# A hybrid decoder layer: the feed-forward products as seven block products in place of eight

## The reference

```python
def _swiglu(h, w_gate, w_up, w_down):
    return (jax.nn.silu(h @ w_gate) * (h @ w_up)) @ w_down

x = x + 1/2 * SwiGLU_1(RMSNorm(x))          # d_ff = 2816
x = x + token_mix(RMSNorm(x))               # RWKV-7 and mLSTM mixers, gates, W_out
x = x + cross_attention(RMSNorm(x), RMSNorm(mem))   # 4 heads, 256 memory tokens
x = x + 1/2 * SwiGLU_2(RMSNorm(x))
out = RMSNorm(x)
```

## Time and profile before

| | us |
|---|---|
| median of 3 runs | 2962.98 |
| the runs | 2962.14, 2962.98, 2966.65 |
| the profiled execution: its span (the page gives no other time for it) | 2967.3 |
| TensorE busy | 2849.2 |
| VectorE, GpSimd, ScalarE busy | 1354.6, 1246.7, 564.3 |
| first part, from the first matmul to its last | 12.3 to about 740.7 |
| second part | 2219.9 to 2939.3 |

### The profile page before, as it was taken

One profiled execution on the slowest core, in us unless ns is written; L12 is line 12 of the kernel. 1 busy time (PEld: TensorE's weight loads), 2 busy tenths in 40 slices (PEclk: granted clock), 3 DMA queues, 4 the chain that ended last, 5 costly groups with the idle time before them and its releaser, 6 DMA issues.

```text
span 2967.3 us, 36791 instructions
## 1 busy us (share of the span) xinstructions
PE 2849.2 (96%) x14694; PEld 2359.7 (80%) x14694; DVE 1354.6 (46%) x1109; ACT 564.3 (19%) x793; POOL 1246.7 (42%) x627
## 2 busy tenths in 40 slices
PE   7999999999999998999999999998899999999996
PEld 5888888888788877777777778888788888888885
DVE  5431331234556535776777555543344322331334
ACT  3100010012000112443444232214321100100011
POOL 3433344433694623555555443321043344433331
PEclk9999999999999999998999999999999999999998
DMA  3111111112762554444434164122011111111111
GB/s 133 43 50 50 50 49 45 48 46 103 298 247 92 192 194 149 101 107 139 102 102 104 61 223 149 51 75 102 8 43 50 49 50 47 46 49 50 50 41 73
DMA packets 115401, 271.35 MB, mean 91 GB/s; under 512 B 7644, under 2 KB 58972, under 8 KB 108272
## 3 DMA queue, kind: packets, MB, share of 16 engines
q1 hardware_dynamic: 93504, 210.79, 22.4%
q10 hardware_dynamic: 21808, 59.27, 5.3%
HBM read 207.56 MB, written 62.44 MB: 91 GB/s over the span
## 4 chain that ended last, share of the span: by engine, by line
PE 79%; issue 9%; POOL 6%; DVE 4%; ACT 1%; DMA 0%; SPq 0%; POOLq 0%; DVEq 0%; ACTq 0%
PE G L755 24%; PE G L757 24%; PE G L756 24%; PE G L879 2%; POOL AL L686 2%; PE G L1164 1%; PE G L916 1%; POOL Tr L680 1%; ACT sx L1559 0%; DVE nt_a L1644 0%; DVE mx L2008 0%; DVE px L2016 0%; POOL rho L669 0%; PE G L1156 0%; PE G L820 0%
## 5 line engine op out<-in xcount | busy, mean ns | idle before, releaser
L719 POOL TENSOR_TENSOR whi<-raw,zero 128x1024 fp32r<-128x1024 f32 (+1 forms) x199 | 378.2, 1900 | 1312.8 <-PE G L757 1233.2
L755 PE MATMUL G<-hhi,whi 128*128 128x512 f32 x2032 | 794.0, 391 | 21.0 <-DVE hlo L1650 17.9
L757 PE MATMUL G<-hhi,wlo 128*128 128x512 f32 x2032 | 791.8, 390 | 0.0
L756 PE MATMUL G<-hlo,whi 128*128 128x512 f32 x2032 | 791.5, 390 | 0.0
L722 POOL TENSOR_TENSOR wlo<-raw,whi 128x1024 fp32r<-128x1024 f32 (+1 forms) x199 | 482.6, 2425 | 15.6
L755 PEld LDWEIGHTS G<-hhi,whi 128*128 128x128 f32 x2032 | 382.1, 188 | 104.2 <-issue 13.0
L757 PEld LDWEIGHTS G<-hhi,wlo 128*128 128x128 f32 x2032 | 382.1, 188 | 79.8
L756 PEld LDWEIGHTS G<-hlo,whi 128*128 128x128 f32 x2032 | 382.2, 188 | 79.6 <-issue 0.7
L755 PE MATMUL G<-ahi,whi 128*128 128x512 f32 x960 | 374.8, 390 | 2.7 <-DVEq L457 2.7
L756 PE MATMUL G<-alo,whi 128*128 128x512 f32 x960 | 374.2, 390 | 0.0
L757 PE MATMUL G<-ahi,wlo 128*128 128x512 f32 x960 | 374.1, 390 | 0.0
(11 more groups left out here) (329 smaller groups left out, 3301.8 us busy)
## 6 DMA issues: line engine op xcount, KB each, us to landing
gw<-gw_d SPq DMA_DIRECT2D x32, 1024.0 KB, 5.3
raw<-in_wg SPq DMA_DIRECT2D x44, 512.0 KB, 3.2
raw<-in_wu SPq DMA_DIRECT2D x44, 512.0 KB, 3.3
raw<-in_wd SPq DMA_DIRECT2D x32, 512.0 KB, 3.3
gw_d<-gw SPq DMA_DIRECT2D x16, 1024.0 KB, 4.8
graw<-in_gates_in SPq DMA_DIRECT2D x16, 512.0 KB, 7.2
raw<-in_ml_in SPq DMA_DIRECT2D x16, 512.0 KB, 3.7
zml_d<-po ACTq DMA_DIRECT2D x16, 512.0 KB, 2.6
```

The costliest lines, as they stand in the source:

```text
L719: nc.gpsimd.tensor_tensor(whi[:, k, 0:w], raw[:, k, 0:w], zero[:].to_broadcast([P, w]), ALU.add).then_inc(hi_made, 1)
L755: nc.tensor.matmul(dst, wh, hi, start=start, stop=False)
L756: nc.tensor.matmul(dst, wh, lo, start=False, stop=False)
L757: return nc.tensor.matmul(dst, wl, hi, start=False, stop=stop)
```

## The change

Both feed-forward parts are rewritten; the rest is as it was, but for places of tiles and semaphores. Weights and tokens are cut into 2 x 2 blocks: a pair of output columns by a pair of input tiles for the weights (A11 to A22), a pair of input tiles by two halves of 512 tokens for the tokens (B11 to B22). Four block products of two terms each, eight products, become seven, of sums of blocks (the Winograd form of Strassen's scheme):

- weights: S1 = A21 + A22, S2 = S1 - A11, S3 = A11 - A21, S4 = A12 - S2, made by GpSimd (`sums`);
- tokens: T1 to T4, sums of the B blocks, made once a part by VectorE in the place of `xT`, and split into high and low like the rest (`opT`; B11, B21 and B22 are in `opB`);
- products: P1 = A11 B11, P2 = A12 B21, P3 = S4 B22, P4 = A22 T4, P5 = S1 T1, P6 = S2 T2, P7 = S3 T3. P1, P6, P7 and P4 follow one another in one PSUM bank, P5 and P3 in a second, P2 in a third; what is read in between is copied out by ScalarE (`pp1`, `pu2`, `pp5`). c11 = P1 + P2, c12 = (P1 + P6) + P5 + P3, c22 = (P1 + P6 + P7) + P5, c21 is what the first bank holds at the end.

The work goes by slots: 22 for gate and up (even: the gate of 256 columns of d_ff, odd: their up; each product has 4 tiles), then 24 for down (six parts of the d_ff pairs, `PARTS`, one pair in the first part and two in the others, times four pairs of output chunks). A slot's weights are one load of 1 MB for gate and up. Each weight block has one buffer: ScalarE rounds the high part after the slot before has used it, VectorE makes the low part (in down GpSimd does). The activations of a pair are seven tiles (three blocks and four sums), split into high and low, and are stored in DRAM (`act_d`, 1.8 MB each of high and low) and loaded again for down in time for their part, except for the last pair's. x is loaded again too (`tokens_back`), since T1 to T4 overwrote it; the second part stores it before.

The diff is cut to SP's and GpSimd's program, TensorE's order, ScalarE's high part and the copy of U2, and VectorE's low part, one down step and its order of work:

```diff
-FF_PARTS = (8, 8, 6)
+PAIRS = FFC // 2
+HK = KD // 2
+NA = 2 * PAIRS
+PARTS = (((0, 0),), ((1, 2), (10, 3)), ((2, 0), (3, 1)), ((4, 2), (5, 3)), ((6, 0), (7, 1)), ((8, 2), (9, 3)))
+NB = len(PARTS) * (KD // 2)
...
+    act_d = [dram(f"act_d{f}", [PAIRS, 2, P, 7, HALF]) for f in range(2)]
...
+            def pair_weights(g):
+                if g < NA:
+                    dst, src = flat(sraw[g % 2][:]), (wu if g % 2 else wg)[g // 2]
+                else:
+                    p, m = divmod(g - NA, HK)
+                    w = len(PARTS[p]) * P
+                    dst, src = rsum[g % 2][:, 0:4, 0:w], wd[p][m].rearrange("p (b c) -> p b c", b=4)
+                sp.dma_start(dst, src).then_inc(sraw_in[g % 2], 16)
+
+            def slot(q, n):
+                for part, dst in enumerate((slh[n], sll[n])):
+                    sp.dma_start(dst[:].rearrange("p b t -> p (b t)").bitcast(F32),
+                                 act_d[f][q, part].rearrange("p b t -> p (b t)")).then_inc(slot_in[n], 16)
+
+            def tokens_back(m):
+                sp.dma_start(xT[:, 2 * m:2 * m + 2, :], x_src[:, 2 * m:2 * m + 2, :]).then_inc(xs_in[m], 16)
+
...
+            for g in range(NA - 1):
+                sp.wait_ge(*w_lo.at(f"A22_{g}", f))
+                sp.wait_ge(sum_made, (n0 + g + 1) * 4)
+                if g + 2 == NA + 1:
+                    break
+                pair_weights(g + 2)
+                if g % 2 == 0 and g:
+                    j = g // 2 - 1
+                    sp.wait_ge(act_hi, f * 2 * PAIRS + 2 * j + 2)
+                    sp.dma_start(act_d[f][j, 0].rearrange("p b t -> p (b t)"),
+                                 flat(hiS[:]).bitcast(F32)).then_inc(hi_out, 16)
+                    sp.wait_ge(act_lo, f * 2 * PAIRS + 2 * j + 2)
+                    sp.dma_start(act_d[f][j, 1].rearrange("p b t -> p (b t)"),
+                                 vS[:, 1:8, :].rearrange("p b t -> p (b t)")).then_inc(lo_out, 16)
+            sp.wait_ge(hi_out, (f + 1) * (PAIRS - 1) * 16)
+            sp.wait_ge(lo_out, (f + 1) * (PAIRS - 1) * 16)
+            tokens_back(0)
+            sp.wait_ge(p_made[1], n0 + NA)
+            sp.wait_ge(p_made[2], n0 + NA)
+            slot(0, 0)
+            sp.wait_ge(p_made[6], n0 + NA)
+            pair_weights(NA + 1)
+            sp.wait_ge(act_made, (f + 1) * 3 * PAIRS - 1)
+            tokens_back(1)
+            sp.wait_ge(p_made[4], n0 + NA)
+            slot(1, 2)
+            sp.wait_ge(act_lo, (f + 1) * 2 * PAIRS)
+            for m in (2, 3):
+                tokens_back(m)
+            for g in range(NA, SLOTS - 2):
+                sp.wait_ge(gw_lo, f * 3 * NB + 3 * (g - NA + 1))
+                pair_weights(g + 2)
+                p, m = divmod(g - NA, HK)
+                if m == 0 and p and p + 1 < len(PARTS):
+                    sp.wait_ge(p_made[4], n0 + g)
+                    for q, n in PARTS[p + 1]:
...
+        def sums(f, g):
+
+            n = f * SLOTS + g
...
+                pool.wait_ge(*w_lo.at(f"S1_{g - 1}", f))
+            tt(d["S1"], r["A21"], r["A22"], ALU.add).then_inc(sum_made, 1)
+            if 0 < g < NA:
+                pool.wait_ge(*w_lo.at(f"S2_{g - 1}", f))
+            pool.wait_ge(sum_made, n * 4 + 1)
+            tt(d["S2"], d["S1"], r["A11"], ALU.subtract).then_inc(sum_made, 1)
+            if 0 < g < NA:
+                pool.wait_ge(*w_lo.at(f"S3_{g - 1}", f))
+            tt(d["S3"], r["A11"], r["A21"], ALU.subtract).then_inc(sum_made, 1)
+            if 0 < g < NA:
+                pool.wait_ge(*w_lo.at(f"S4_{g - 1}", f))
+            pool.wait_ge(sum_made, n * 4 + 2)
+            tt(d["S4"], r["A12"], d["S2"], ALU.subtract).then_inc(sum_made, 1)
+
...
+            for g in range(NA + 1):
+                sums(f, g)
+            for g in range(NA, SLOTS):
+                for n in range(3):
+                    pool.wait_ge(gw_hi, f * 3 * NB + 3 * (g - NA) + n + 1)
+                    src, hi = group(n, 0, g)
+                    tt(group(n, 1, g)[1], src, hi.bitcast(F32), ALU.subtract).then_inc(gw_lo, 1)
+                if g + 1 < SLOTS:
+                    sums(f, g + 1)
...
+            def product(i, g, bank, opens):
+
+                name, x = PRODUCTS[i]
+                if g < NA:
+                    pe.wait_ge(*w_lo.at(f"{name}_{g}", f))
+                    for q in range(HK):
+                        last = resident(i, bank, opens and q == 0, q, q == HK - 1)
+                else:
+                    pe.wait_ge(gw_lo, f * 3 * NB + 3 * (g - NA) + GROUP_OF[name] + 1)
+                    part = PARTS[(g - NA) // HK]
+                    for e, (q, n) in enumerate(part):
+                        at = (g % 2) * 2 * P + e * P
+                        last = piece(i, bank, opens and e == 0, slice(at, at + P), slh[n][:, X_AT[x], :],
+                                     sll[n][:, X_AT[x], :], e == len(part) - 1)
+                last.then_inc(p_made[i], 1)
...
+            for g in range(1, SLOTS):
+                if g >= NA and (g - NA) % HK == 0:
+                    p = (g - NA) // HK
+                    for q, n in PARTS[p]:
+                        if q == PAIRS - 1:
+                            pe.wait_ge(act_lo, (f + 1) * 2 * PAIRS)
+                        else:
+                            pe.wait_ge(slot_in[n], (f * LOADS[n] + LOAD_AT[q]) * 32 + f * 16)
+                first(g)
+                if g == NA - 1:
+                    second(g)
+                if g > 1:
+                    third(g - 1)
+                fourth(g - 1)
+                sixth(g)
+                fifth(g)
+                if g != NA - 1:
+                    second(g)
+                seventh(g)
+            third(SLOTS - 1)
+            fourth(SLOTS - 1)
...
+            def high(name, g):
+
+                i = next(i for i, (x, _) in PRODUCTS.items() if x == name)
+                if g:
+                    act.wait_ge(p_made[i], n0 + g)
+                if name in RAW_AT:
+                    act.wait_ge(sraw_in[g % 2], (f * (SLOTS // 2) + g // 2 + 1) * 16)
+                else:
+                    act.wait_ge(sum_made, (n0 + g) * 4 + {"S1": 1, "S2": 2, "S3": 3, "S4": 4}[name])
+                activation(stationary(name, 0), unsplit(name, g), ACT.Copy).then_inc(*w_hi.sig(f"{name}_{g}"))
...
+            def u2_copy(g):
+                act.wait_ge(p_made[6], n0 + g + 1)
+                act.wait_ge(c12_made, n0 + g)
+                if g == 0:
+                    act.wait_ge(root_made, f * 2 + 1)
+                activation(pu2[:], bank_b(g), ACT.Copy).then_inc(u2_read, 1)
+
...
+            def low(name, g):
+
+                dve.wait_ge(*w_hi.at(f"{name}_{g}", f))
+                tt(stationary(name, 1), unsplit(name, g), stationary(name, 0).bitcast(F32),
+                   ALU.subtract).then_inc(*w_lo.sig(f"{name}_{g}"))
...
+            for n, x in enumerate(T_ORDER):
+                dve.wait_ge(t_hi, f * HK + n + 1)
+                stt(opT[:, T_AT[x], 1], raw_t(x), -1.0 if x == "T1" else 1.0, opT[:, T_AT[x], 0].bitcast(F32), ALU.mult,
+                    ALU.subtract).then_inc(t_lo, 1)
+            root(flat(G[0][:]), nrx_f[:])
+            dve.wait_ge(root_made, f * 2 + 1)
+            dve.wait_ge(t_lo, (f + 1) * HK)
+            for g in range(NA):
+                j, up = divmod(g, 2)
+                more = g + 1 < NA
+                if up:
+                    gate_22(j)
+                elif j:
+                    up_22(j - 1)
+                if g:
+                    low("S3", g)
+                if more:
+                    low("A11", g + 1)
+                if up:
+                    scaled(j, 0)
+                elif j:
+                    up_12(j - 1)
+                if g:
+                    low("S4", g)
+                if not up and j:
+                    up_21(j - 1)
+                if g:
+                    low("A22", g)
+                if up:
+                    gate_12_21(j)
+                    scaled(j, 1)
+                elif j:
+                    differences(j - 1)
+                if more:
+                    low("S2", g + 1)
+                if up:
+                    scaled(j, 2)
+                elif j:
+                    act_low(j - 1, 0, hiS, None)
+                if more:
+                    low("S1", g + 1)
+                if up:
+                    up_11(j)
+                else:
+                    if j:
+                        act_low(j - 1, 1, hiS, None)
+                    gate_11(j)
+                if more:
+                    low("A12", g + 1)
+            for g in range(NA, SLOTS):
+                j = PAIRS - 1
+                if g == NA:
+                    up_22(j)
+                    down_1(g)
+                    up_12(j)
+                    up_21(j)
+                    differences(j)
+                    down_2(g)
+                    act_low(j, 0, slh[3], sll[3])
+                    down_3(g)
+                    act_low(j, 1, slh[3], sll[3])
```

(7 more changed lines are left out.)

683 lines of the change are left out of this document (562 added, 121 removed).

## The result

| | us |
|---|---|
| the changed kernel, median of 4 runs | 2949.58 (2946.10 to 2956.97) |
| the kernel before, 4 runs beside them | 2964.82 (2962.14 to 2968.21) |
| ratio | 0.9947, 95% interval 0.9929 to 0.9965 |
| span of the profiled execution | 2955.2, forecast 2891.3 |
| forecast of the time | 2887, range 2842 to 2938 |

A forecast was written before the change was run, and what follows sets the result against it. TensorE's matmul stream, busy 96% of the span, was taken as the bound. -179.5 + 36.5 + 21.8 + 7 + 32.4 + 4.8 + 1 = -76.0 took the span to 2891.3, the time to 2887; range 2842 to 2938.

The forecast's parts named there:

- The matmuls removed: Both feed-forward parts: 396 fewer matmuls each, 792 at 0.2267 us, -179.5 us.
- Entries: Slot 0 of each part: TensorE waits for VectorE's chain of sums, low parts and root; +36.5 and +21.8 us.
- Gate and up, steady: Gate and up slots: VectorE fits, P4 waits for c22 by 0.3 us a pair, 22 pairs, +7 us.
- The two rivals in which it sets the pace: VectorE sets gate and up: mildly, 2 us a pair, 2924 (0.12); fully, slower than before, 3052 (0.07).
- the one in which products drain: Feed-forward parts: 644 products each drain 0.16 us, +103 us, slower than before, 2990; chance 0.03.
- From up to down: Slots 22 to 24: waits of 4.5 us for activations and 11.7 for queued weights, 16.2 a part, +32.4 us.
- Down, steady: Down slots: engines fit; a part's fourth-slot weights, queued behind activations, come at 29.4 against 28.6, three times a part, +4.8.
- Tail: End of each part: the last two chunks come together, a square and a sum more than half hidden, +1 us.
- Consts, the parking of tokens and the mixers' first weights move within covered time: Between the parts: these transfers and weights cost nothing, since the projection's first product takes chunks 0 to 5 first.
- 354 GB/s: Rival: loads at the rate of the stretch with stores lengthen waits at the transition and fourth slots; 2921, chance 0.12.

The follow-up runs named there:

- e6_halves: Changed kernel with GpSimd's split of the mixers' first weights delayed and VectorE's step for the next norm in two one-chunk halves; 2951.23 us, ratio 0.9944.
- e4_trans: Changed kernel with slot 24's weight load issued once its buffer is free, ahead of the wait for the last activations and two token loads; 2943.00 us, ratio 0.9912.

## Why the prediction was wrong in size

By its own terms the miss of 64 is: tail 20.6, down 18.9, from up to down 14.4, between the parts 13.2 (forecast 0), gate and up 1.3, entries -3.9.

*The matmuls removed* (-179.5): right, 13902 against 14694, at 0.2267 wherever nothing waits.

*Entries* (+36.5, +21.8): right within 3.3 and 0.6 us. In the first part the chain ran as forecast and a little shorter: VectorE's T sums end at 49.0 (50.8 forecast), their low parts at 59.9 (61.6), the root at 67.0 (68.8), and P7 waits for U2's copy:

```profile
67.80 0.50 PE L960 MATMUL G<-opT,wA 128*128 128x512 f32 x1 [2.70 <-ACT pu L1637]
```

The second part's nearness is partly luck. The terms of its sum come to 43.6 in line, and to about 38.1 only if the first (5.6) runs beside the parked copy (6.5), as it did. The parked copy then took longer, so that the sums could begin 10.4 us into the slot (7.1 forecast), and GpSimd, priced at 3.5, met none of the four T sums.

*Gate and up, steady* (+7): right in size, 4.0 and 4.2 us, but not in place. The forecast had 0.3 us a pair of slots at P4, waiting for c22; no such wait is in the trace. There are two waits a part, 1.36 in slot 1 and 0.57 in slot 21, and the rest is spread over 1750 starts. VectorE does fit. The two rivals in which it sets the pace are out, and so is the one in which products drain.

*From up to down* (+32.4): the wait for activations was right (4.10 us, 4.5 forecast, second part 5.0), and so was the place of the next, but not its price. The one wait forecast at 11.7 comes as four (in the first part 3.02, 1.57, 0.36 and 5.99), 10.9 and 11.3 us in all. Slot 24 starts 30.2 us after slot 22, forecast 25.3: SyncE issues pair 1's load 8.6 us into slot 22 (6.3 forecast), its wait for VectorE's last low part holds the tokens and the weights until 496.4, and the weights land 27.6 us into the slot (22.7). Beside the waits 8.2 and 7.4 us are lost, 7.1 and 6.3 of them in slow starts. The failed step is that the clock was priced at the entries only, 3 us each, and nowhere else, though the earlier trace rows showed the half speed behind an idle TensorE.

*Down, steady* (+4.8): mis-sized fivefold (measured 23.7), in three ways. The load of slot 29's weights did take the forecast time, 29.6 us from slot 26's start to the resumed matmuls (29.4 forecast), but it was due after 27.4 (549.17 less the wait of 2.19 and the start at 519.6), not 28.6, since slot 26 begins with two short products of slot 25. At slots 33, 37 and 41 of the first part it was due after 28.7 and came after 31.0, 30.3 and 30.3. So the waits are 1.4 to 2.35 each in place of 0.8, they come at four slots of a part, not three (7.5 and 7.8 us in all), and behind four of the eight the clock drops (3.1 and 2.9 us in the two parts, of the 4.2 and 4.2 lost beside the waits).

*Tail* (+1): failed most for its size, 17.5 and 4.1. The step priced the last pair of chunks behind the last slot and didn't ask what the other three, put between the adds of slots 43 to 45, do to TensorE: a slot lasts 9.5 us, VectorE's adds and this step together 9.3 even alone (7 x 0.61, twice 1.2 and 1.3), and GpSimd, which begins its next work at that moment, stretches it in the first part. In the second part, whose step has only the sums and no GpSimd beside it, two halves leave 0.1 us (e6_halves); what the first part would lose without that neighbour no run shows.

*"Consts, the parking of tokens and the mixers' first weights move within covered time"*: failed, 0 forecast, 13.2 measured. The code puts the parking of tokens behind a DMA that waits for the root, and for the queue's next store VectorE already waited 17.4 us in the kernel before. The cover was taken for granted and rests on no row.

The rivals didn't hold the outcome either: the loads were not at 354 GB/s. Two stretches of the load behind which slot 29 waits:

```profile
530.00:535.00 5.00, 5.00 (x23) 4.13 (x23) 2.33 (x5) 1.48 (x2) 4.99 (x4) 1.00 1.01 433
535.00:540.00 5.00, 5.00 (x23) 4.13 (x22) 2.54 (x4) 0.00 (x0) 0.00 (x0) 1.00 1.00 426
```

The Trainium skill (DMA: Bandwidth & Descriptors, Specifications) gives about 358 GB/s for one core; the measured 433 decides, and the size of the miss doesn't come from there.

## What to carry to other kernels

A DMA queue's order is a dependence: put a large transfer that is needed late one piece at a time behind the small ones that are needed soon, and look at what stands behind each new wait on every issuing engine, also outside the changed stretch. Where a stream has been without gaps, give a wait its length and allow for a half-speed stretch behind it: here 65.9 us of waits brought 24.6 of it, spread unevenly, since the shorter waits often brought none. Ask of every engine not whether its work fits a slot's sum but whether the longest piece in one place fits the room between two dependent products, and who is its neighbour then.

## What the runs showed of the hardware

That TensorE falls to its lower clock level behind a wait of 2.19 us (549.17, half speed from 550.47 to 553.46) was not expected; nor that behind 2.81 us (e4_trans, 2740.69) it doesn't. The length of the wait alone doesn't decide it in these rows.

VectorE's slowness beside GpSimd depends on its operands. Its adds in the down products, which read one operand from PSUM, run beside GpSimd's work in every slot and are never slowed; its instructions with two operands in SBUF are, as 713.50 above:

```profile
L2285 DVE SCALAR_TENSOR_TENSOR xT<-G,xT 128x512 f32<-128x512 f32 x336 | 229.9, 690 | 229.6 <-PE G L962 229.6
```

The mean of 336 is 690 ns, what one takes alone. The Trainium skill (SBUF — State Buffer, SBUF: two separate sides) states just this lock between a VectorE instruction with two SBUF inputs and a GpSimd instruction that reads SBUF, and the trace agrees.
